# Order of work at three joints of a hybrid encoder kernel: scan entry, last routed tile, second expert block

## The chip, the core and the metric

The kernel runs on one core of a Trainium2 chip. A core has five engines with an instruction stream each: PE (TensorE, matrix products into PSUM), DVE (VectorE), ACT (ScalarE), POOL (GpSimd), and SP (SyncE), which here only issues DMA transfers. They meet through semaphores. All transfers are carried by the core's 16 DMA engines; SP's go through one queue (q1), POOL's indirect gathers and scatters through another (q0). The metric is device time in microseconds, the median of several executions, less is better.

## The reference

Two batches, of 1024 and 512 tokens with 1024 features in float32, pass one layer each with shared weights; the kernel treats them as 1536 tokens in 12 tiles of 128.

```python
def _forward(x, ...):
    h = _rms_norm(x, norm1_w)
    u = h @ w_in
    y_a = _rwkv7_mixer(shifted u, ...)        # 8 heads x 64, both directions
    y_b = _hgrn2_mixer(u, lb, gnorm_w)        # 4 heads x 128, both directions
    x = x + concat(y_a, y_b) @ w_out
    h2 = _rms_norm(x, norm2_w)
    x = x + _hier_moe(h2, ...)
    return _rms_norm(x, final_norm_w)

# hgrn2, per direction, chunks of 32 steps
    G = jnp.cumsum(g_c, axis=-2)
    o = A @ v_c + (q_c * jnp.exp(G)) @ S      # A: decayed scores inside a chunk
    S = jnp.exp(G_last)[..., None] * S + (k_c * jnp.exp(G_last - G)).T @ v_c

# hier_moe
    glog = h @ wg + bg ; grp = argmax(glog)
    elog = h @ we + be ; top_v, top_i = top_k(elog of that group, 2)
    # rows sorted by expert into blocks of 128, then for each block
    hid = silu(xb @ w_gate[e]) * (xb @ w_up[e]) ; yb = hid @ w_down[e]
    # gate-weighted sum of the two experts of each token
```

## The kernel before

It is one program in stages. First the input projection of the RWKV columns, with norm and token shift. Then `mix_rwkv_project_hgrn`: the RWKV recurrence over 48 chunks of 32 steps (iteration `c` of `steps()`), interleaved on PE with the projection of the HGRN2 columns. This stage is a block of its own: its five engine programs end together, and the next block's begin together. The next block is `mix_hgrn_project_out` with the routing and, without another such border, `experts_and_final_norm`.

**The scan entry.** At the end of the RWKV block SP loads the chunks' decays (`scan_decay`) and the first tile's keys and queries (`kq_first`) back from DRAM; DVE makes the products of decays of the HGRN2 scan (`upto`, `to2`, `to3`) and the first tile's scaled keys (L1540 to L1566). The scan itself goes over 12 tiles with index `c`, for two directions `d`. Its steps are `prep` (DVE scales keys), `scores` (PE), `turn_k` (PE turns the keys, ACT copies them), `grow` (PE multiplies keys by values, DVE adds this to the state) and `out` (PE, two products for each of four heads, into `o_ps_o`). Each engine runs its own version of the step. `schedule` fixes one order for all engines, and `gap(c, budget)` puts pieces of other work (`fillers`: norms, gates, output projection, routing) between them: r_ names belong to the RWKV half, n_ names to the norm of heads, `half` to the output projection, and `turn`, `routed`, `choose`, `rank`, `place` to the router.

**The last routed tile.** A finished tile n (order `FINISHED`) goes through: `half` x 4 (two column halves of `ps_out`, two parts of the sum), `x1_half` (DVE adds the residual), `x1` (ACT squares), `msq`, `m_root`, `h2n` (DVE scales the tile by the root and the norm weight into `work`), `turn` x 2 (PE turns it through `ps_x`, ACT copies to `h2T`), `routed` (PE, eight products with the router weights; DVE adds the bias). For each pair g of tiles `choose` picks the experts, `weigh` makes the exponentials, `rank` counts on PE and `place` gives each row its slot. POOL scatters the tokens to the `slots`. After the last pair a single product with the matches gives the first block's row indices (`first_idx`).

**The expert blocks.** Block b takes 128 rows x[b % 2]. PE does gate (L2858), down of block b-1 (L2867), up (L2858). Weights are double-buffered: wg, wu, wd with index b % 2. Those of expert 0 and the gate weights of expert 1 are loaded when the scan ends. SP loads up and down of expert 1 after the first rows have landed (`e_first_row`), then goes through a loop in which each load waits for PE's last use of its buffer. POOL gathers rows: it waits for the scattered slots, loads the tokens of the block, and issues four indirect gathers of a quarter row each; DVE turns the block (L2971).

## Time and profile before

| | us |
|---|---|
| median of 3 runs | 2351.63 (2350.96 to 2352.99) |
| the profiled execution | 2347.96 |
| its span in the trace | 2346.1 |
| PE busy in the span | 2228.4 (95%) |
| DVE, ACT, POOL busy | 1032.1, 713.7, 407.5 |
| mean granted clock of TensorE | 0.978 of full speed |

The span is cut by the stages: RWKV projection to 360, RWKV recurrence to 1230, scan with output projection and routing to 1622, experts to 2318, final norm to the end. "Granted clock" is the share of TensorE's full 2.4 GHz; 0.5 is 1.2 GHz. In timelines a row is a run of equal instructions on one engine: start, length, what it is, and in brackets how long the engine was idle before it and whose work ended that idle time. A matmul in float32 leaves two records, so x8 are four matmuls.

### The profile page before, as it was taken

How to read it: one execution, taken by the hardware profiler on the slowest of the kernel's cores; microseconds unless marked ns; L12 is line 12 of the kernel's file. 1: busy time of each engine (PE TensorE's matmuls, PEld its weight loads, DVE VectorE, ACT ScalarE, POOL GpSimd, SP SyncE). 2: the span in 40 equal slices, each digit the busy share in tenths (PEclk: the TensorE clock that was granted, in tenths of full speed). 3: DMA queues.
4: the chain of work that ended last, by engine and by line, in shares of the span. 5: the costliest groups of instructions: out<-in, count | busy, mean ns of one | idle time of the engine just before them, and what ended most of it. 6: DMA issues, size and time to landing. Idle time of an engine off the chain costs nothing. (4 is left out here: it accounts for less than half of the span.)

```text
span 2346.1 us, 64499 instructions
## 1 busy us (share of the span) xinstructions
PE 2228.4 (95%) x28004; PEld 1463.3 (62%) x28004; DVE 1032.1 (44%) x2219; ACT 713.7 (30%) x1441; POOL 407.5 (17%) x506
## 2 busy tenths in 40 slices
PE   7999999999999999999998989998799999999996
PEld 4444444445555555555557756656688888888884
DVE  3336776834644744644655766644111111111114
ACT  4124454623544544544542322221000000000003
POOL 1012222310000000000002210102533333333321
PEclk9999999999999999999997999997899999999998
DMA  4103344443343333333338843454799999999997
GB/s 142 36 23 126 135 157 139 171 106 92 92 111 83 99 97 93 93 96 91 88 108 243 260 147 117 158 180 146 252 362 353 331 355 334 361 352 334 362 330 290
DMA packets 359966, 436.66 MB, mean 186 GB/s; under 512 B 164994, under 2 KB 296198, under 8 KB 351536
## 3 DMA queue, kind: packets, MB, share of 16 engines
q1 hardware_dynamic: 343232, 397.94, 50.0%
q0 software_dynamic: 14384, 35.19, 6.1%
q8 instruction: 192, 3.15, 0.6%
q10 hardware_dynamic: 2112, 0.01, 0.1%
q14 instruction: 46, 0.38, 0.0%
HBM read 329.84 MB, written 104.50 MB: 185 GB/s over the span
## 5 line engine op out<-in xcount | busy, mean ns | idle before, releaser
L1198 PE MATMUL h_pp<-hT,r_wcol 128*128 128x512 f32 x832 | 413.0, 619 | 3.3 <-ACT h_iraw L1313 3.3
L2858 PE MATMUL e_ps_gu<-e_xT,e_wg 128*128 128x128 f32 x2048 | 236.4, 277 | 12.6 <-DVE e_xT L2971 12.6
L2858 PEld LDWEIGHTS e_ps_gu<-e_xT,e_wu 128*128 128x128 f32 x2048 | 233.6, 192 | 14.3 <-issue 14.3
L2858 PEld LDWEIGHTS e_ps_gu<-e_xT,e_wg 128*128 128x128 f32 x2048 | 233.5, 194 | 13.2 <-DVE e_xT L2971 12.8
L2858 PE MATMUL e_ps_gu<-e_xT,e_wu 128*128 128x128 f32 x2048 | 233.8, 275 | 0.0
L2867 PE MATMUL e_ps_y<-e_wd,e_hid 128*128 128x512 f32 x512 | 225.1, 592 | 0.7 <-DVE e_hid L3030 0.7
L1198 PEld LDWEIGHTS h_pp<-hT,r_wcol 128*128 128x128 f32 x832 | 141.5, 189 | 124.0 <-issue 108.8
L522 PE MATMUL h_pp<-hT,r_wcol 128*128 128x512 f32 x480 | 215.2, 607 | 1.3 <-DVE hT L794 1.3
L2983 DVE TENSOR_SCALAR e_y<-e_ps_y,e_row 128x512 f32<-128x512 f32 x31 | 23.3, 751 | 337.7 <-PE e_ps_y L2867 337.6
L522 PEld LDWEIGHTS h_pp<-hT,r_wcol 128*128 128x128 f32 x480 | 92.6, 195 | 113.7 <-issue 112.0
L2867 PEld LDWEIGHTS e_ps_y<-e_wd,e_hid 128*128 128x128 f32 x512 | 94.8, 190 | 108.7 <-issue 107.1
L2922 ACT ACTIVATE e_silu<-e_ps_gu 128x512 f32<-128x512 f32 x31 | 18.5, 597 | 424.2 <-PE e_ps_gu L2858 424.2
L2255 PE MATMUL o_ps_out<-o_wout,y 128*128 128x512 f32 x288 | 130.6, 600 | 4.0 <-DVE y L2469 4.0
L2651 POOL DMA_INDIRECT e_x<-h,e_idx x128 | 124.6, 973 | 55.6 <-issue 29.3
L2010 POOL MEMSET g_mask<- 128x256 f32 x1 | 0.3, 311 | 736.8 <-POOLq L1058 736.8
L1375 ACT ACTIVATE m_v<-m_ps_x 32x256 f32<-32x256 f32 x192 | 72.0, 375 | 148.9 <-PE m_ps_x L1258 147.2
L2990 DVE TENSOR_TENSOR e_hid<-e_ps_gu,e_silu 128x512 f32<-128x512 f32 x31 | 21.4, 690 | 196.9 <-PE e_ps_gu L2858 196.9
L776 POOL TENSOR_TENSOR r_spans<-r_spans 128x512 f32<-128x512 f32 x24 | 42.0, 1770 | 375.5 <-DVE r_spans L866 375.5
L522 PE MATMUL r_pp<-hT,r_wcol 128*128 128x512 f32 x240 | 105.4, 592 | 0.0
L2255 PEld LDWEIGHTS o_ps_out<-o_wout,y 128*128 128x128 f32 x288 | 53.0, 192 | 60.7 <-issue 60.7
L522 PEld LDWEIGHTS r_pp<-hT,r_wcol 128*128 128x128 f32 x240 | 45.4, 190 | 56.4 <-issue 56.4
L2918 ACT ACTIVATE e_y<-e_ps_y,e_row 128x512 f32<-128x512 f32 x31 | 21.3, 687 | 185.8 <-PE e_ps_y L2867 185.8
(419 smaller groups left out, 3406.7 us busy)
## 6 DMA issues: line engine op xcount, KB each, us to landing
e_wg<-in_moe_w_gate_dram SPq DMA_DIRECT2D x32, 2048.0 KB, 12.6
e_wu<-in_moe_w_up_dram SPq DMA_DIRECT2D x32, 2048.0 KB, 12.8
e_wd<-in_moe_w_down_dram SPq DMA_DIRECT2D x32, 2048.0 KB, 12.7
r_wcol<-in_w_in_dram SPq DMA_DIRECT2D x35, 512.0 KB, 5.5
ar<-r_ar SPq DMA_DIRECT2D x24, 512.0 KB, 2.7
kb<-r_kb SPq DMA_DIRECT2D x24, 512.0 KB, 2.8
m_ar<-ar SPq DMA_DIRECT2D x48, 256.0 KB, 4.7
m_kb<-kb SPq DMA_DIRECT2D x48, 256.0 KB, 3.5
```

The lines of the kernel that those rows point to most:

```text
L522: last = nc.tensor.matmul(pp[k % SPANS][:], wcol[q][:, c], self.hT[:, c, s * SPAN:(s + 1) * SPAN], start=c == 0, stop=c == KT - 1)
L776: nc.gpsimd.tensor_tensor(gx[d][:], gi[d][:], sg[d][:], ALU.subtract).then_inc(*pool_aux.inc(f"gx{d}"))
L1198: last = nc.tensor.matmul(pp[n % 2][:], wcol[(k + 2) % 3][:, c], self.hT[:, c, span(s)], start=c == 0, stop=c == KT - 1)
L1375: last = nc.scalar.activation(out, ps_ru[quad[q]], ACT.Copy)
L2255: last = nc.tensor.matmul(ps_out[:, h * SPAN:(h + 1) * SPAN], y[:, k, tile(FINISHED[n])], wout[:, k, h * SPAN:(h + 1) * SPAN], start=k == ...
L2651: self.nc.gpsimd.indirect_dma_start(self.e_x[u][:, g], None, self.h2.rearrange("t (q e) -> (t q) e", q=4), bass.IndirectOffsetOnAxis(ap=se ...
L2858: last = nc.tensor.matmul(ps[:, q * P:(q + 1) * P], w[u][:, c, q * P:(q + 1) * P], xT[u][:, c * P:(c + 1) * P], start=c == 0, stop=c == KT ...
L2867: last = nc.tensor.matmul(ps_y[:, n * 512:(n + 1) * 512], hid[u][:, q * P:(q + 1) * P], wd[u][:, q, n * 512:(n + 1) * 512], start=q == 0, ...
L2918: return nc.scalar.activation(y[u][:, 0:512], ps_y[:, 0:512], ACT.Copy, scale=gate[u])
L2922: made = nc.scalar.activation(silu[:], ps_g, ACT.Silu)
L2983: return nc.vector.tensor_scalar(y[u][:, 512:], ps_y[:, 512:], gate[u], None, ALU.mult)
L2990: made = nc.vector.tensor_tensor(hid[u][:], ps_u, silu[:], ALU.mult)
```

## The change

Four edits.

1. The scan entry moves forward. SP's loads stand in `load_entry`, called right behind the last stores of keys and decays, ahead of later stores. DVE's instructions stand in `enter_scan`, called in the last chunk's iteration ahead of the last addition to the state.
2. At the scan's start, `prep(1)` stands ahead of the second `turn_k`, and the first tile's two `out` steps stand in front of the second `scores`. PE waits for the clearing of `ps_s` before its first scores, no longer at the block's top.
3. The order of the fillers for tile index 11 is written out in `endings()`. The last tile is not scaled by its root before it is turned: DVE multiplies each half by the norm weight as soon as it is added, and the root scales the logits in the instruction that adds the bias; ACT squares the halves apart (DVE adds the two sums) and scales `work` for the store of h2. After the scan the second half of each `turn` goes through `ps_k`, and `routed` begins when the first half is copied.
4. SP waits for the second block's rows as well before it loads up and down of expert 1.

```diff
+                    def load_entry():
+                        for u in range(2):
+                            sp.wait_ge(kq_stored[u], 16 * 3 * PAIRS)
+                            sp.wait_ge(dc_stored[u], 16 * PAIRS)
+                        sp.dma_start(scan_decay[:], self.hdecay.rearrange("d j p c -> p (d j) c")).then_inc(scan_decay_loaded, 16)
+                        for i in range(2):
+                            sp.dma_start(kq_first[:, i], self.kq.rearrange("d j two p t -> p two (d j) t")[:, i, :, 0:P]
+                                         ).then_inc(self.kq_loaded[0], 16)
...
                             if it == whole(m) + 5:
                                 store_kq(m, 2)
                                 store_dc(m)
+                                if m == 2 * PAIRS - 1:
+                                    load_entry()
...
+                    def enter_scan():
...
+                        nc.vector.memset(to3[:], 1.0).then_inc(spread, 1)
+                        eng.wait_ge(scan_decay_loaded, 16)
...
+                        if c == CHUNKS - 1:
+                            enter_scan()
                         if has_c:
                             self.waits(eng, pe_c.at("MO", c))
...
-                for n in range(-2, TILES + 3):
+                for n in range(-2, TILES - 1):
...
+                return out + endings()
+
+            def endings():
+
+                e, g = TILES - 1, LAST_PAIR - 1
+                return [(name, args, cost, e) for name, args, cost in (
+                    ("turn", (e - 2, 0), 1.1), ("rank", (g - 1,), 0.4), ("half", (e, 0, 0), 3.5), ("place", (g - 1,), 0),
+                    ("msq", (e - 1,), 0), ("m_root", (e - 1,), 0), ("turn", (e - 2, 1), 1.1), ("routed", (e - 2,), 1.7),
+                    ("h2n", (e - 1,), 0), ("half", (e, 1, 0), 3.5), ("choose", (g, 0), 0), ("turn", (e - 1, 0), 1.1),
+                    ("choose", (g, 1), 0), ("turn", (e - 1, 1), 1.1), ("half", (e, 0, 1), 3.5), ("routed", (e - 1,), 1.7),
+                    ("x1_half", (e, 0), 0), ("choose", (g, 2), 0), ("weigh", (g,), 0), ("half", (e, 1, 1), 3.5),
+                    ("x1_half", (e, 1), 0), ("x1", (e,), 0), ("msq", (e,), 0), ("rank", (g,), 0.4), ("turn", (e, 0), 1.1),
+                    ("turn", (e, 1), 1.1), ("m_root", (e,), 0), ("place", (g,), 0), ("h2n", (e,), 0), ("routed", (e,), 1.7))]
...
+                run("prep", 1)
                 run("turn_k", 0, 1)
+                run("out", 0, 0)
                 run("grow", 0, 1)
-                run("prep", 1)
                 gap(-1, 1.0)
+                run("out", 0, 1)
...
+            turn_bank = lambda n, h: bank_k if ("turn", n, h) in bank_k.use else bank_x
...
-                self.waits(eng, bank_x.done(("turn", n, 1)), bank_y.free(("logits", n)), (params, 16 * 5))
+                self.waits(eng, bank_y.free(("logits", n)), (params, 16 * 5))
                     for c in range(KT):
+                        if c % PAIRS == 0:
+                            self.waits(eng, turn_bank(n, c // PAIRS).done(("turn", n, c // PAIRS)))
...
+                def routed(n):
+                    if n == LAST:
+                        self.waits(eng, dve_t.at("inv", n))
+                        nc.scalar.activation(work[n % RING_X][:], work[n % RING_X][:], ACT.Copy, scale=rq[:, n:n + 1]
+                                             ).then_inc(*act_last.inc("h2"))
...
+                    if n == LAST:
+                        half = slice(h * SPAN, (h + 1) * SPAN)
+                        self.waits(eng, dve_x.at("x1" if h else "low", n))
+                        nc.vector.tensor_tensor(by_k(work[u][:, half]), hgrn(t) if h else rwkv(n), by_k(n2w[:, half]), ALU.mult
+                                                ).then_inc(*dve_last.inc("high" if h else "low"))
...
+                    if n == LAST:
+                        self.waits(eng, dve_t.at("inv", n))
+                        nc.vector.scalar_tensor_tensor(self.logits[:, FINISHED[n]], ps_y[:, 0:NG + NE], rq[:, n:n + 1], rbias[:],
+                                                       ALU.mult, ALU.add).then_inc(bank_y.read, 1)
+                        return
...
-                self.waits(sp, (self.e_first_row, 16))
+                self.waits(sp, (self.e_first_row, 16), (x_loaded[1], 64))
                 self.load_up(sp, 1, 1)
                 self.load_down(sp, 1, 1)
```

How this moves instructions on the engines, at three places. On DVE at the end of the RWKV block (`m_grown` and `m_state` are the addition to the last chunk's state; `g_to`, `g_upto`, `h_first` the scan entry), before:

```order
L1517 TENSOR_TENSOR m_xt<-m_px,m_ps_b 128x128
L1497 TENSOR_TENSOR m_grown<-m_ps_x,m_state 128x2x4x64
L1500 TENSOR_TENSOR m_state<-m_grown,m_decay 128x512
L1540 MEMSET g_to 128x384
L1542 MEMSET g_decay 128x8
L1544 COPY g_upto<-g_decay 128x96
```

And the end of the same stretch in the changed kernel:

```order
L1509 TENSOR_TENSOR h_first<-h_first,g_to 128x1024
L1512 TENSOR_TENSOR g_upto<-g_upto,g_decay 128x96
L1514 TENSOR_TENSOR g_upto<-g_upto,g_decay 128x96
L1516 TENSOR_TENSOR g_upto<-g_upto,g_decay 128x96
L1536 TENSOR_TENSOR m_grown<-m_ps_x,m_state 128x2x4x64
L1539 TENSOR_TENSOR m_state<-m_grown,m_decay 128x512
L1058 UNCONDITIONAL_BRANCH
```

The addition to the state is now the last work of the block, and the 14 instructions of the entry stand in front of it. On PE at the start of the scan (`e_wu`, `e_wg`, `e_wd` are the expert buffers, which hold values, state and keys during the scan; numbers are buffers), before, from the last first-tile scores on:

```order
L2200 MATMUL o_ps_s<-h_first 128x32 x8
L2214 MATMUL o_ps_k<-e_wu0,e_wg1 128x128 x4
L2207 MATMUL o_ps_k<-ident,h_first 128x128 x4
L2214 MATMUL o_ps_k<-e_wu0,e_wg1 128x128 x4
L2192 MATMUL o_ps_s<-e_wg0 32x32 x3
```

And after:

```order
L2231 MATMUL o_ps_s<-h_first 128x32 x8
L2245 MATMUL o_ps_k<-e_wu0,e_wg1 128x128 x4
L2238 MATMUL o_ps_k<-ident,h_first 128x128 x4
L2255 MATMUL o_ps_o<-e_wu0,e_wd0 128x128
L2257 MATMUL o_ps_o<-e_wg1,e_wu0 128x128
L2255 MATMUL o_ps_o<-e_wu0,e_wd0 128x128
L2257 MATMUL o_ps_o<-e_wg1,e_wu0 128x128
L2255 MATMUL o_ps_o<-e_wu0,e_wd0 128x128
L2257 MATMUL o_ps_o<-e_wg1,e_wu0 128x128
L2255 MATMUL o_ps_o<-e_wu0,e_wd0 128x128
L2257 MATMUL o_ps_o<-e_wg1,e_wu0 128x128
L2245 MATMUL o_ps_k<-e_wu0,e_wg1 128x128 x4
```

The first output (eight matmuls) stands between the second turn of the keys and the second growth; eight more for the other direction follow this growth, ahead of the second scores. On PE at the end of the routing (`o_ps_out` the output projection, `o_ps_y` logits and ranks, `o_ps_x` and `o_ps_k` turned halves), before:

```order
L2255 MATMUL o_ps_out<-o_wout,y 128x512 x8
L2264 MATMUL o_ps_x<-ident,o_x 128x128 x4
L2255 MATMUL o_ps_out<-o_wout,y 128x512 x8
L2271 MATMUL o_ps_y<-o_wr,o_top 128x36 x8
L2264 MATMUL o_ps_x<-ident,o_x 128x128 x8
L2271 MATMUL o_ps_y<-o_wr,o_top 128x36 x8
L2264 MATMUL o_ps_x<-ident,o_x 128x128 x4
L1680 MATMUL o_ps_y<-q_picked,q_strict 128x64
L1681 MATMUL o_ps_y<-q_before,allsum 128x64
L2264 MATMUL o_ps_x<-ident,o_x 128x128 x4
L2271 MATMUL o_ps_y<-o_wr,o_top 128x36 x8
```

And after:

```order
L2286 MATMUL o_ps_out<-o_wout,y 128x512 x4
L2296 MATMUL o_ps_k<-ident,o_x 128x128 x4
L2305 MATMUL o_ps_y<-o_wr,o_top 128x36 x8
L2286 MATMUL o_ps_out<-o_wout,y 128x512 x4
L2296 MATMUL o_ps_x<-ident,o_x 128x128 x4
L2296 MATMUL o_ps_k<-ident,o_x 128x128 x4
L2286 MATMUL o_ps_out<-o_wout,y 128x512 x4
L2305 MATMUL o_ps_y<-o_wr,o_top 128x36 x8
L2286 MATMUL o_ps_out<-o_wout,y 128x512 x4
L1688 MATMUL o_ps_y<-q_picked,q_strict 128x64
L1689 MATMUL o_ps_y<-q_before,allsum 128x64
L2296 MATMUL o_ps_x<-ident,o_x 128x128 x4
```

The router products and turns of the two tiles before stand between the projection's halves instead of behind them; only a turn of `o_ps_k` and the last router product follow these rows.

## Rows read from the trace of the kernel before

**Rows 1.** By stretch: us, busy of each engine (instructions), PE clock, DMA share, GB/s.

```profile
1300.00:1596.00 296.00, 281.03 (x1874) 187.83 (x1868) 176.78 (x464) 80.68 (x172) 37.77 (x34) 0.99 0.52 165
1600.30:1622.10 21.80, 17.83 (x84) 16.48 (x83) 14.28 (x78) 5.02 (x12) 4.65 (x12) 0.57 0.21 74
1657.35:2318.00 660.65, 660.06 (x4470) 540.14 (x4470) 115.04 (x113) 53.22 (x90) 233.71 (x304) 1.00 0.93 338
```

**Rows 2.** Timeline of DVE at the scan entry: start, length, work [idle before <-releaser].

```profile
1222.69 0.69 DVE L1497 TENSOR_TENSOR m_grown<-m_ps_x,m_state 128x512 f32<-128x512 f32 x1 [6.51 <-PE m_ps_x L1271]
...
1224.14 0.38 DVE L1540 MEMSET g_to<- 128x384 f32 x1
...
1228.81 0.33 DVE L1566 TENSOR_TENSOR g_upto<-g_upto,g_decay 128x96 f32<-128x96 f32 x1
```

**Rows 3.** Timeline of SP at the scan entry.

```profile
1205.70 0.47 SPq L1136 DMA_DIRECT2D hdecay<-h_dc  x1
...
1216.60 0.37 SPq L1170 DMA_DIRECT2D g_decay<-hdecay  x1
...
1227.76 0.34 SPq L1125 DMA_DIRECT2D hgate<-h_gst  x1
```

**Rows 4.** Timeline of PE in the first tiles of the scan.

```profile
1237.43 1.44 PE L2214 MATMUL o_ps_k<-e_wu,e_wg 128*128 128x128 f32 x8 [0.39 <-DMA e_wu<-itok]
1240.08 1.11 PE L2207 MATMUL o_ps_k<-ident,h_first 128*128 128x128 f32 x4 [1.22 <-DVE e_wg L2419]
1241.88 2.07 PE L2214 MATMUL o_ps_k<-e_wu,e_wg 128*128 128x128 f32 x8 [0.69 <-ACT e_wg L2302]
1247.29 0.33 PE L2192 MATMUL o_ps_s<-e_wg 128*32 128x32 f32 x6 [3.33 <-issue]
...
1255.27 0.63 PE L2224 MATMUL o_ps_o<-e_wu,e_wd 128*128 128x128 f32 x2
...
1258.64 1.06 PE L2214 MATMUL o_ps_k<-e_wu,e_wg 128*128 128x128 f32 x8
```

**Rows 5.** Timeline of PE near the end of the routing.

```profile
1584.36 7.09 PE L2255 MATMUL o_ps_out<-o_wout,y 128*128 128x512 f32 x16
...
1598.59 1.87 PE L2271 MATMUL o_ps_y<-o_wr,o_top 128*128 128x36 f32 x16
```

**Rows 6.** Timeline of DVE at the end of the routing.

```profile
1598.86 0.69 DVE L2481 TENSOR_TENSOR y<-o_ps_out,o_x 128x512 f32<-128x512 f32 x1 [2.74 <-PE o_ps_out L2255]
...
1608.49 0.23 DVE L1696 TENSOR_TENSOR q_pos<-o_ps_y,q_region 128x64 f32<-128x64 f32 x1 [1.21 <-PE o_ps_y L1681]
...
1610.84 0.16 DVE L1724 TENSOR_TENSOR q_token<-q_token,q_e 128x2 f32<-128x2 f32 x1
...
1614.00 0.16 DVE L1619 TENSOR_REDUCE q_gmax<-logits 128x2 f32<-128x8 f32 x1
```

**Rows 7.** Timelines of DVE and PE at the second expert block.

```profile
1655.28 2.01 DVE L2971 STREAM_TRANSPOSE e_xT<-e_x 128x1024 f32<-128x1024 f32 x1 [24.56 <-DMA e_x<-h,e_idx]
...
1657.35 9.31 PE L2858 MATMUL e_ps_gu<-e_xT,e_wg 128*128 128x128 f32 x64 [12.60 <-DVE e_xT L2971]
...
1680.51 7.31 PE L2858 MATMUL e_ps_gu<-e_xT,e_wg 128*128 128x128 f32 x64
```

**Rows 8.** Timelines of POOL and SP ahead of it.

```profile
1634.84 2.08 POOL L2639 DMA_DIRECT2D e_tok<-slots  x3 [6.20 <-DMA slots<-q_token,dest]
1641.36 0.18 POOL L2644 COPY e_row<-e_tok 128x4 uint32<-128x4 uint32 x1 [4.44 <-DMA e_tok<-slots]
...
1626.88 0.33 SPq L2615 DMA_DIRECT2D e_wu<-in_moe_w_up_dram  x1
```

**Rows 9.** Landings: slots 1550:1620; rows 1640:1648; rows 1657.5:1664.

```profile
DMA to landing us min/median/max: 2.1/2.1/4.1
...
DMA to landing us min/median/max: 4.4/7.0/8.6
...
DMA to landing us min/median/max: 2.7/2.7/2.7
```

More of the change, by code:

```diff
@@ L1975, in schedule @@
                     gap(c - 1, budget)
-                    run("out", c, 0)
+                    if c:
+                        run("out", c, 0)
                     if more:
@@ L1981, in schedule @@
                         run("turn_k", c + 1, 1)
[L1982 removed]
+                    if c:
+                        run("out", c, 1)
                     if c + 2 < TILES:
@@ L2099, in load_x @@
                         if n >= EARLY:
-                            self.waits(sp, bank_x.full(("turn", n - RING_X, 1)), (h2_stored[u], n // RING_X * 16))
+                            self.waits(sp, turn_bank(n - RING_X, 1).full(("turn", n - RING_X, 1)), (h2_stored[u], n // RING_X * 16))
                         elif n >= RING_X:
@@ L2352, in turn @@
                 def turn(n, h):
-                    self.waits(eng, bank_x.full(("turn", n, h)), bank_y.full(("logits", n - 1)))
-                    nc.scalar.activation(h2T[:, h * SPAN:(h + 1) * SPAN], ps_x[:], ACT.Copy).then_inc(bank_x.read, 1)
-                schedule(turn_k=turn_k, out=out, n_sq=n_sq, n_root=n_root, n_wide=n_wide, r_evict=r_evict, x1=x1, m_root=m_root, turn=turn,
+                    self.waits(eng, turn_bank(n, h).full(("turn", n, h)), bank_y.full(("logits", n - 1)))
+                    nc.scalar.activation(h2T[:, h * SPAN:(h + 1) * SPAN], turn_ps(n, h), ACT.Copy
+                                         ).then_inc(turn_bank(n, h).read, 1)
+                def routed(n):
[3 more added lines that the diff above has]
+                                             ).then_inc(*act_last.inc("h2"))
+                schedule(turn_k=turn_k, out=out, n_sq=n_sq, n_root=n_root, n_wide=n_wide, r_evict=r_evict, x1_half=x1_half, x1=x1, m_root=m_root, turn=turn, routed=routed,
                          weigh=lambda g: self.weigh(eng, g))
```

113 lines of the change are left out of this document (62 added, 51 removed).

## The prediction

> **What bounds the kernel now.** I read the page first: PE is busy 95% of the span, so a change can only give time where PE waits, or where it runs at half of its clock. Then I read PE's timeline and the waits of three places, and for each place the engine that ends the wait. After 1657.35 the expert loop runs without a hole: 660.06 of 660.65 us busy at a granted clock of 1.00, that is 2.4 GHz, with the DMA engines at a share of 0.93 [rows 1]. The change touches three joints ahead of this loop.
>
> *Scan entry, 1227 to 1260.* DVE prepares the scan from 1224.14 to 1229.14 [rows 2]; SP's last issue of the old block ends at 1228.10 [rows 3]. The new block starts after that. PE then sits idle 1.22, 0.69 and 3.33 us between 1238.87 and 1247.29, 5.24 in all, and the same eight matmuls of L2214 take 2.07 us at 1241.88 and 1.06 at 1258.64: the first at 1.2 GHz, the second at 2.4 [rows 4].
>
> *End of the routing, 1599 to 1622.* PE is busy up to 1600, then at a mean clock of 0.57 [rows 1]. The last half of x1 is added at 1598.86, and DVE begins to choose the last pair's experts at 1614.00 [rows 6]: 14.45 us after that addition's end at 1599.55.
>
> *Second block's rows, 1644 to 1657.* PE ends the first up projection at 1644.75 and stands 12.60 us until the second block's rows are turned; the gate projection then takes 9.31 us where one in the loop takes 7.31 [rows 7]. The rows are late because each link of POOL's chain lands slowly: 6.20 us of waiting for the scattered slots, 4.44 for the tokens [rows 8], up to 8.6 for the gather [rows 9]. SP has the weights of expert 1, two transfers of 2.1 MB, in flight since 1626.88 [rows 8].
>
> **The sum, part by part.**
>
> *Entry: 4.5 us.* The same instructions stand on DVE, ahead of the last addition of the state. DVE was free there: it waited 6.51 us until 1222.69 [rows 2], so from 1216.18. The entry is 5.00 us long and would end at 1221.2, 1.5 us before it hurts. Its three loads move on SP's queue from behind the gate store (1216.60) to behind the last store of the decays (issued by 1206.17) [rows 3]; the next issue on that queue came 10 us later, so they land before DVE comes to them and hold nothing up. What ends last now is SP at 1228.10, so the block turns over 1.04 us sooner. PE no longer waits for the clearing before its first turn; that is worth nothing, since growing the state waits for the value rows, which land with 0.39 us of idle as the end of the chain [rows 4]. Then the order: the first outputs, eight pairs of matmuls, go into the holes. One such output took 3.37 us at half clock (1255.27 to 1258.64), the other half as long again at full clock, 1.8: 5.2 us leave the stretch behind the second scores. In front, with the 1.04 us taken off: growth ends at 1237.8, turn 1.22 later until 1240.1, output to 1243.5, growth 2.07 to 1245.6, second output 3.4 more to 1249.0; the scores begin 1.7 us later than at 1247.29. Net 3.5 at half clock throughout. Moving the scaling of the second keys ahead of the second growth is what permits it: DVE does it while PE outputs. If the dense outputs raise the clock early, as 128-wide matmuls did from 1255.27 on, the second output takes 1.8 and the gain is 5.1; the scores and the turn before 1255.27 fill 8 us at half clock, and if most of that halves too, 8.6. Against this stands the DMA, which fills that stretch. I take 4.5, near the lower case; ends 1.0 (the turnover alone) and 8.6.
>
> *End: 6.1 us.* PE's work before the last half of x1 is the same four halves of the projection (16 records in 7.09 us, two halves; 6.87 without the overlap at the end, so 3.44 each) and one turn of 0.45. Two router products of 1.7 (1.87 less the same overlap) [rows 5] and two more turns, which stood behind them, now stand between them. So the last projection ends at 1584.36 + 4 x 3.44 + 3 x 0.45 + 2 x 1.7 = 1602.9 instead of 1598.8. DVE adds (0.69) and multiplies by the norm weight (0.69): 1604.3. PE turns both halves at once, into two banks, unscaled. ACT squares the last half (by my estimate 0.6 with the sum behind it), then copies the two turns, loads its table and takes the root; DVE meanwhile places the older pair, 2.5 us (1608.49 to 1611.00 before) [rows 6], from 1604.9 to 1607.4, and I take the root to be there by then. One reciprocal and the scaled logits follow, 0.4: choosing begins at 1607.9 instead of 1614.00. The 2 x 0.69 on DVE and the whole-tile scaling on ACT are new; the latter feeds only the store of h2, which the first gather reads when choosing and ranking are over, as now. Ends: 4.0, if the root comes 2 us behind the placement; 7.5, if PE's clock, 0.57 in the mean there [rows 1], also stays up through the small products behind.
>
> *Rows before weights: 14.6 us.* SP now waits for the second rows before it issues expert 1's up and down weights. POOL's chain then meets idle DMA engines. I use the quiet landings, 2.1 us for slots and 2.7 for rows [rows 9]: POOL is free at 1628.64 (1634.84 - 6.20), slots there at 1630.7, tokens at 1633.5 (with 2.7 again), and the 13.92 us from 1641.36 to 1655.28 shrink by 8.6 - 2.7 to 8.0: rows there at 1641.5, turned 2.0 later at 1643.5 [rows 7, 8]. PE's up projection ends at 1644.75. So the wait goes whole, 12.60, and with it the cold start, 9.31 - 7.31 = 2.0. What is late next? SP's weights, issued at 1641.5 instead of 1626.9. The up weights are wanted after gate and down, 1644.75 + 7.15 + 6.87 = 1658.8; 2.1 MB at the loop's 338 GB/s [rows 1] take 6.2 us. The next gate weights stand behind 6.8 MB in all: 20.1 us, 1661.6, wanted at 1665.9. Later ones have more time. Queued behind SP's new wait are those loads only. Ends: 8.7, if the gather still lands in 8.6; 14.6, since no more hole is left.
>
> This case's landings speak to a rule. A gather took 4.4 to 8.6 us beside the weights and 2.7 alone [rows 9]. The Trainium skill, DMA: Bandwidth & Descriptors, section Queues, rings and completion order, says each DMA engine goes round-robin between queue rows at packet granularity; read strictly, a small transfer then never stands behind the whole 4 MB, and holding the weights back gives the rows little. By the rule the third term is near 0; by the rows it is 14.6. The trace bears the interleaving out in so far as the gather did land long before the weights' 4 MB were through, yet three times later than alone.
>
> All three move in a line (the second joint starts later work only by its own sum), and the entry's gain passes 1300 to 1596, where PE is busy all but 15 us of 296 [rows 1]. 4.5 + 6.1 + 14.6 = 25.2. The profiled execution took 2347.96 (span 2346.1), so 2322.8. It stood 3.67 below the median of the three runs, 2351.63; against that median I predict 2326.4.
>
> **Rivals.**
> *Entry absorbed:* the stretch is held by transfers (the value rows are the releaser at 1237.43), and the reordered outputs only move idle time. Entry 1.0, total 21.7: 2329.9.
> *Rows still late:* POOL's chain is slow for its own reasons, or packets interleave anyway. For it: POOL's own issues and three round trips are in it. Against: the quiet landings. Third term 0, total 10.6: 2341.0.
> *Weights late, slower:* the loop is transfer-bound at a share of 0.93, and the time in which no weights are issued never comes back. Place: the up weights of the second block and all behind them. If the rows came as late as 1655.28, issue slips by 28.4 us; less 10.6 that gives +17.8: 2369.4. It decides once the weights' lateness eats more than 10.6 us. Against it: PE lost 0.6 us in 660 at that share [rows 1].
> *Change not effective:* the entry's loads land late, DVE holds up the last state and the block; that costs what it exceeds 1.5 us by, at most about 3: 2326.4 + 7.5 = 2333.9.
>
> **Chances.** Forecast 0.66, entry absorbed 0.20, rows late 0.08, entry held up 0.03, weights late 0.03. The likeliest case alone ranges from 2321 to 2333. The range with eight in ten, 2320 to 2336, takes in the absorbed entry and a gather that lands half as slowly; it leaves out the late rows and late weights. 0.2% is 4.7 us, about what a measurement of this kernel can tell from no change. All cases but one are faster by more: faster 0.96, same 0.02, slower 0.02.
>
> **What would show it.** Entry: DVE's scan preparation ends near 1221, PE's holes of 1.22 and 3.33 are one of 1.2, and the second scores start between 1247 and 1249. End: from the last addition of x1 to the choosing, 4.3 us instead of 14.45. Rows: no PE idle before the second gate projection, that projection at 7.31, slots and tokens landing in 2 to 3 us. It is wrong if PE shows a wait on expert weights in the loop, if the gather still lands in over 6 us, or if PE's holes reappear between 1260 and 1300.

## The result and the profile after

| | before | changed |
|---|---|---|
| median of 4 runs, us | 2351.30 (2346.73 to 2352.99) | 2319.53 (2315.62 to 2324.88) |
| profiled execution, us | 2347.96 | 2317.24 |
| its span, us | 2346.1 | 2315.7 |
| mean granted clock of TensorE | 0.978 | 0.984 |

The ratio of the medians is 0.9869, with a 95% interval of 0.9843 to 0.9896: 24.5 to 36.9 us faster. The forecast was 2326.4 us, with a range of 2320 to 2336; the median lies 0.5 us under the low end. Two things have to be told apart: what the edits moved, and why the total is larger than that.

**Three joints.** I cut both traces at the same instructions. The scan stretch runs from the end of the last projection of the block before to the first half projection of the last tile; the end stretch from there to the choosing of the last pair's experts; the rows stretch from there to the first down projection of the experts.

| stretch, us | before | changed | gained | forecast |
|---|---|---|---|---|
| ahead of the scan | 1227.10 | 1221.72 | 5.38 | 0 |
| scan | 357.26 | 351.58 | 5.68 | 4.5 |
| end | 29.64 | 23.90 | 5.74 | 6.1 |
| rows | 52.49 | 38.61 | 13.88 | 14.6 |
| from there to the end | 679.62 | 679.84 | -0.22 | 0 |

The edits' stretches give 25.3 us where the forecast had 25.2. Most of the surplus is the first row. Here are the windows of both kernels up to the last projection (columns: stretch, its length, PE busy with its instructions, PE clock, DMA share, GB/s). First before:

```profile
0.00:1227.10 1227.10, 1182.44 (x20736) 0.99 0.37 104
```

then the changed kernel:

```profile
0.00:1221.70 1221.70, 1179.96 (x20736) 0.99 0.37 104
```

The same 20736 instructions, 2.5 us less of busy time and 2.9 us less of idle time. The first moved instruction in this stretch is SP's load of the decays, at 1203.01 in the changed kernel. Here is one group of 32 of PE's records well ahead of it, before and then changed:

```profile
1193.31 1.10 PE L1217 MATMUL m_ps_s<-m_ar,m_kb 64*64 64x128 f32 x32
```

```profile
1187.78 1.10 PE L1221 MATMUL m_ps_s<-m_ar,m_kb 64*64 64x128 f32 x32
```

The changed kernel is 5.53 us ahead there, and 5.38 at the end of the stretch. So the lead was there before any edited instruction ran, and the moved ones added nothing to it.

**Scan entry** [rows 2 to 4]. DVE's timeline in the changed kernel (start, length, work, [idle before <-releaser]):

```profile
1210.83 0.38 DVE L1490 MEMSET g_to<- 128x384 f32 x1
...
1215.52 0.33 DVE L1516 TENSOR_TENSOR g_upto<-g_upto,g_decay 128x96 f32<-128x96 f32 x1
1217.38 0.69 DVE L1536 TENSOR_TENSOR m_grown<-m_ps_x,m_state 128x512 f32<-128x512 f32 x1 [1.53 <-PE m_ps_x L1275]
```

The preparation takes 5.0 us and leaves 1.53 us before the state's last addition; 1.5 was forecast. SP's last old issue and its first new one:

```profile
1222.38 0.34 SPq L1125 DMA_DIRECT2D hgate<-h_gst  x1
1223.25 0.59 SPq L2106 DMA_DIRECT2D y<-ytok  x1
```

That store still ends last, as forecast. PE in the first tiles:

```profile
1223.28 0.63 PE L2238 MATMUL o_ps_k<-ident,h_first 128*128 128x128 f32 x4 [1.56 <-PEq L1058]
...
1230.74 2.05 PE L2245 MATMUL o_ps_k<-e_wu,e_wg 128*128 128x128 f32 x8 [2.02 <-DMA e_wu<-itok]
1234.00 1.12 PE L2238 MATMUL o_ps_k<-ident,h_first 128*128 128x128 f32 x4 [1.22 <-DVE e_wg L2470]
...
1236.62 0.45 PE L2255 MATMUL o_ps_o<-e_wu,e_wd 128*128 128x128 f32 x2
...
1237.58 1.06 PE L2245 MATMUL o_ps_k<-e_wu,e_wg 128*128 128x128 f32 x8
...
1241.60 1.12 PE L2228 MATMUL o_ps_s<-e_wg 128*64 128x32 f32 x16
...
1250.69 1.11 PE L2264 MATMUL o_ps_x<-ident,o_wide 128*128 128x128 f32 x4 [1.88 <-DVE o_wide L2503]
```

The holes of 0.69 and 3.33 us of [rows 4] are filled. The clock rises inside the first output (0.45 instead of 0.63 us for a matmul), so the second growth takes 1.06 and the second scores start at 1240.5: 18.75 us after the last projection's end, where the kernel before took 20.19 and I had forecast 20 to 22. The value rows are now waited for, 2.02 us, and a new hole of 1.88 stands at 1250.69.

**End of the routing** [rows 5, 6]. DVE, and then PE's last half projection:

```profile
1592.31 0.69 DVE L2532 TENSOR_TENSOR y<-o_ps_out,o_x 128x512 f32<-128x512 f32 x1 [0.95 <-PE o_ps_out L2286]
1593.04 0.69 DVE L2537 TENSOR_TENSOR o_x<-y,o_top 128x512 f32<-128x512 f32 x1
...
1596.39 0.16 DVE L1732 TENSOR_TENSOR q_token<-q_token,q_e 128x2 f32<-128x2 f32 x1
1596.62 0.16 DVE L2551 RECIPROCAL o_rq<-o_rq 128x1 f32<-128x1 f32 x1
1596.92 0.26 DVE L2562 SCALAR_TENSOR_TENSOR logits<-o_ps_y,o_rq,o_rbias 128x36 f32<-128x36 f32 x1
1597.21 0.16 DVE L1627 TENSOR_REDUCE q_gmax<-logits 128x2 f32<-128x8 f32 x1
```

```profile
1588.53 3.68 PE L2286 MATMUL o_ps_out<-o_wout,y 128*128 128x512 f32 x8
```

From the addition's end to the choosing 4.2 us; 4.3 was forecast, 14.45 stood there before. The reciprocal follows the placing of the older pair without a wait: the root had been ready.

**Second block's rows** [rows 7 to 9]. POOL, SP, DVE and PE in the changed kernel:

```profile
1613.29 2.08 POOL L2706 DMA_DIRECT2D e_tok<-slots  x3 [1.43 <-DMA slots<-q_token,dest]
1615.47 0.18 POOL L2711 COPY e_row<-e_tok 128x4 uint32<-128x4 uint32 x1
```

```profile
1623.60 0.33 SPq L2682 DMA_DIRECT2D e_wu<-in_moe_w_up_dram  x1
```

```profile
1623.53 2.04 DVE L3038 STREAM_TRANSPOSE e_xT<-e_x 128x1024 f32<-128x1024 f32 x1 [9.54 <-DMA e_x<-h,e_idx]
```

```profile
1628.67 7.31 PE L2925 MATMUL e_ps_gu<-e_xT,e_wg 128*128 128x128 f32 x64
1635.82 7.03 PE L2934 MATMUL e_ps_y<-e_wd,e_hid 128*128 128x512 f32 x16
1642.69 7.31 PE L2925 MATMUL e_ps_gu<-e_xT,e_wu 128*128 128x128 f32 x64
```

The wait for the slots fell from 6.20 to 1.43, that for the tokens from 4.44 to nothing; the slots' landing, from one tile's view of 1605 to 1616:

```profile
DMA to landing us min/median/max: 2.1/2.1/2.1
```

The rows are turned at 1625.6, 3.1 us before PE wants them. The windows of the changed kernel for the end of the routing and for the loop (busy of PE, weight load, DVE, ACT and POOL with their instructions, then clock, DMA share, GB/s) show the same pace of the loop as in [rows 1], at a slightly higher share of DMA:

```profile
1583.60:1605.40 21.80, 16.66 (x90) 12.19 (x88) 13.43 (x68) 9.07 (x17) 4.64 (x12) 0.84 0.16 50
...
1628.67:2287.60 658.93, 658.15 (x4473) 538.22 (x4471) 115.24 (x115) 53.44 (x90) 235.55 (x307) 1.00 0.96 352
```

### The profile page after: what moved, and what is told of

Same layout as the page of the kernel before. It is cut to its first block and busy times, and to the rows that moved or that the text cites. A ratio compares the mean times of both kernels' runs of the same rounds, so it can differ in the third digit from the quotient of the medians.

```text
span 2315.7 us, 64509 instructions
## 1 busy us (share of the span) xinstructions
PE 2215.1 (96%) x28004; PEld 1453.8 (63%) x28004; DVE 1032.3 (45%) x2221; ACT 717.5 (31%) x1446; POOL 407.9 (18%) x506
## 5 line engine op out<-in xcount | busy, mean ns | idle before, releaser
L2989 ACT ACTIVATE e_silu<-e_ps_gu 128x512 f32<-128x512 f32 x31 | 18.5, 597 | 410.3 <-PE e_ps_gu L2925 396.6
```

## The experiments

All were timed beside the kernel before, in four sessions (1 to 4, 5 to 8, 9 to 11, and 12; the kernel before had medians of 2350.24, 2347.85, 2346.57 and 2350.60 there); each ratio is to the kernel before of its session. A profile is one execution; in experiments 3, 4 and 8 it was the slowest of its kernel. "Scan", "end" and "rows" are the stretches above in the profiled execution, and "lead" is the end of the last projection ahead of them.

| run | median, us | ratio (95%) | lead | scan | end | rows |
|---|---|---|---|---|---|---|
| before, first profile | 2351.30 | 1 | 1227.10 | 357.26 | 29.64 | 52.49 |
| changed, first profile | 2319.53 | 0.9869 (0.9843 to 0.9896) | 1221.72 | 351.58 | 23.90 | 38.61 |
| 1 changed again | 2319.99 | 0.9881 (0.9861 to 0.9900) | 1222.45 | 352.54 | 23.90 | 38.88 |
| 2 weights first | 2336.24 | 0.9948 (0.9929 to 0.9966) | 1228.77 | 353.22 | 23.90 | 51.05 |
| 3 outputs back | 2326.68 | 0.9901 (0.9883 to 0.9919) | 1227.92 | 363.21 | 23.90 | 38.35 |
| 4 preparation back | 2322.04 | 0.9883 (0.9865 to 0.9900) | 1228.67 | 355.39 | 23.90 | 37.88 |
| 5 endings back | 2326.57 | 0.9909 (0.9884 to 0.9934) | 1224.32 | 356.43 | 28.46 | 37.43 |
| 6 before, rows first | 2334.45 | 0.9949 (0.9932 to 0.9967) | 1221.11 | 361.62 | 29.61 | 37.76 |
| 7 up weights first | 2325.39 | 0.9904 (0.9879 to 0.9930) | 1223.33 | 353.90 | 23.90 | 42.30 |
| 8 values first | 2323.08 | 0.9894 (0.9867 to 0.9920) | 1230.24 | 356.96 | 23.90 | 37.53 |
| 9 fill rows | 2321.10 | 0.9888 (0.9863 to 0.9914) | 1223.72 | 353.04 | 23.90 | 38.64 |
| 10 fill both | 2323.85 | 0.9894 (0.9865 to 0.9924) | 1225.99 | 352.39 | 23.90 | 38.69 |
| 11 fill scan | 2322.43 | 0.9899 (0.9872 to 0.9925) | 1221.49 | 354.64 | 23.90 | 37.97 |
| 12 whole entry back | 2330.62 | 0.9913 (0.9883 to 0.9944) | 1228.19 | 356.81 | 23.90 | 38.54 |

**1, the changed kernel again** (no edit).

> The changed kernel once more, unedited. In its first profile the three joints gave 5.7 (scan entry), 5.7 (end of routing) and 13.9 us (second block's rows), 25.3 in all, and 5.4 us more stood ahead of the first edited instruction: the last projection of the block before the scan ended 5.38 us earlier on the span's clock. Theory A (those 5.4 us are scatter of a single execution): in this profile the three joints give 5 to 6, 5 to 6 and 13 to 15 again, the 5.4 comes out as any number between -4 and +6, and the median stands 24 to 28 us below the kernel before. Theory B (the edits speed the program up from its start, by where its code or its tiles lie): the last projection is again 5 us early, and the median stands 30 to 32 us below.

The joints came out as 4.7 (357.26 - 352.54), 5.7 and 13.6 us. The lead was again early, 1222.45, and the median 30.3 us under the kernel before, which by itself spoke for theory B. The later runs overturned it. Experiments 2 and 3 have the same instructions up there and led at 1228.77 and 1227.92; experiment 6, which is the kernel before up to its expert block, led at 1221.11. The four leads without the moved preparation have a mean of 1226.3, the ten with it 1225.0, each scattering over 7 us or more. Whole executions of one kernel differ as much: 2344.23 to 2354.41 us for the kernel before where it was timed beside experiments 1 to 4. Theory A; a part of 1.3 us, the difference of the means, can't be told from nothing.

**2, weights first.**

```
-                self.waits(sp, (self.e_first_row, 16), (x_loaded[1], 64))
+                self.waits(sp, (self.e_first_row, 16))
```

> The changed kernel with one wait taken back: SP issues expert 1's up and down weights after the first row again. Forecast's theory (bytes in flight slow the small transfers): slots, tokens and gather land in some 6, 4.4 and 4.4 to 8.6 us again, PE stands 12 us before the second gate projection and runs it in 9.3 us: 13.9 us slower than the changed kernel. Rival (packets interleave between queue rows, the small ones never stand behind 4 MB, and the gain came from elsewhere): within 2 us of the changed kernel.

POOL and PE in its trace:

```profile
1626.92 2.08 POOL L2706 DMA_DIRECT2D e_tok<-slots  x3 [6.37 <-DMA slots<-q_token,dest]
1632.66 0.18 POOL L2711 COPY e_row<-e_tok 128x4 uint32<-128x4 uint32 x1 [3.66 <-DMA e_tok<-slots]
```

```profile
1647.91 9.20 PE L2925 MATMUL e_ps_gu<-e_xT,e_wg 128*128 128x128 f32 x64 [10.41 <-DVE e_xT L3038]
```

The rows stretch is 12.4 us longer than in the changed kernel (13.9 was expected), the median 16.3 above experiment 1 of the same session. The forecast's theory holds, the rival falls.

**3, outputs back.** The changed kernel's first-tile order undone:

```
                 run("grow", 0, 0)
-                run("prep", 1)
                 run("turn_k", 0, 1)
-                run("out", 0, 0)
                 run("grow", 0, 1)
+                run("prep", 1)
                 gap(-1, 1.0)
-                run("out", 0, 1)
...
-                    if c:
-                        run("out", c, 0)
+                    run("out", c, 0)
...
```

> The changed kernel with the first tile's two outputs and the scaling of the second keys back in their old places; the moved scan entry stays. The scan entry's joint gave 5.7 us in the first profile. Theory A (holes and clock: the outputs fill PE's 1.2 and 3.3 us of waiting and raise the clock early): 4.7 us slower than the changed kernel, with holes of 1.2 and 3.3 us and the second scores at half clock in the trace. Theory B (transfers hold the stretch until 1280, the outputs only move idle time): under 1.5 us slower.

The median is 6.7 us above experiment 1. The waits of PE in the 80 us behind the last projection (engine, line, <- waited for: us in total, times, longest) begin with the hole that the outputs had filled:

```profile
PE o_ps_s L2219 <- issue: 4.5, 2, 3.3
...
PE o_ps_k L2241 <- DMA e_wu<-itok: 1.7, 1, 1.7
```

In the changed kernel there is no wait before the scores but 0.7 us at the block's start.

Theory A in kind, with the second scores at half clock as it says. The scan stretch of this execution, 363.21, overstates it: the profiled execution was the slowest of its runs (2334.81 us), and experiment 12 shows the same order at 356.81.

**4, preparation back.** The three loads and DVE's preparation stand again behind the loop; the outputs stay moved:

```
-                        if c == CHUNKS - 1:
-                            enter_scan()
...
-                                if m == 2 * PAIRS - 1:
-                                    load_entry()
```

> The changed kernel with the scan entry (DVE's preparation and its three loads) back behind the loop of the block before; the outputs stay moved. Theory A (the entry is worth the turnover alone): 1.0 us slower than the changed kernel, 7.1 us instead of 6.1 from the start of the last projection matmul to the scan's first load on SP. Theory B (the later turnover is absorbed by the value rows, which PE waits for): 0 to 0.3 us, since these rows are issued by the block's own first instructions that is unlikely. Theory C (the order of loads around the gate store also mattered): over 2 us.

From the end of the last projection to PE's first turn it took 2.59 us instead of 1.56, which is the 1.0 of theory A. The median is 2.1 us above experiment 1, with intervals that overlap almost whole; by the medians 1.0 cannot be told from 0 or 2. Theory C, over 2 us, is not excluded by them either; a steadier point in the stretch is read below experiment 12.

**5, endings back.** The last tile as every other:

```
-                return out + endings()
+                return out
...
-            LAST = TILES - 1
+            LAST = None
...
-            turn_bank = lambda n, h: bank_k if ("turn", n, h) in bank_k.use else bank_x
+            turn_bank = lambda n, h: bank_x
...
```

> The changed kernel with the last tile treated as every other again (old end order, one bank for the two turns, norm ahead of the turns). Forecast's theory: from the end of the last addition of x1 to the choosing of the last pair 14.4 us instead of 4.2, while the last projection ends some 4 us earlier; net 5.7 us slower than the changed kernel. Rival (the wait moves: without the new order the ranking and the slots hide part of it): under 3 us slower.

The end stretch is 4.6 us longer (28.46 against 23.90), the median 6.6 above experiment 1's 2319.99 of the other session. From addition to choosing 13.3 us, not 14.4: the mean clock over that time was 0.71 there, 0.63 in the kernel before. The rows stretch is 1.2 shorter than in the changed kernel, since the first gate projection ran less of its time at half clock (7.56 us against 8.62); by both stretches together it is 3.4. So the forecast's theory holds in kind, and the rival, under 3 us, misses by little: up to the choosing the edit is worth 4.6 against this run and 5.7 against the kernel before and experiment 6, and a part of that goes again in the first gate projection.

**6, the kernel before with rows first.** The reverse of experiment 2, on the kernel before.

> The kernel before with one wait added: SP issues expert 1's up and down weights only when the second block's rows have landed. Forecast's theory: this part alone is worth what it was worth with the others, 12 to 14.5 us faster than the kernel before, no idle time of PE before the second gate projection, that projection at 7.3 us. Rival (it pays only after the other two edits, since they moved the rows): under 8 us faster.

```profile
1642.96 7.31 PE L2858 MATMUL e_ps_gu<-e_xT,e_wg 128*128 128x128 f32 x64
```

No idle time ahead of it. The rows stretch shrank by 14.7 us (52.49 to 37.76) and the median by 13.4 (2347.85 to 2334.45). The part is worth as much alone as beside the others, within what the runs can tell, and the rival, under 8 us, falls.

**7, up weights first.**

```
-                self.waits(sp, (self.e_first_row, 16), (x_loaded[1], 64))
+                self.waits(sp, (self.e_first_row, 16))
                 self.load_up(sp, 1, 1)
+                self.waits(sp, (x_loaded[1], 64))
                 self.load_down(sp, 1, 1)
```

> The changed kernel with half of the held weights let go: expert 1's up weights (2.1 MB) are issued after the first row, the down weights still wait for the second rows. Theory A (what delays the small transfers is the bytes queued at that moment, about 6 us of transfer for 2.1 MB): the slots land late (wait of 4 to 6 us instead of 1.4), tokens and gather land as in the changed kernel, the rows are turned 3 to 4 us later, which the up projection just covers: 0 to 1.5 us slower than the changed kernel. Theory B (any weight transfer in flight slows every link, whatever its size): rows 8 us late or more, over 5 us slower. Theory C (packets interleave, nothing is delayed): no link changes.

```profile
1622.07 2.08 POOL L2706 DMA_DIRECT2D e_tok<-slots  x3 [6.30 <-DMA slots<-q_token,dest]
1624.38 0.18 POOL L2711 COPY e_row<-e_tok 128x4 uint32<-128x4 uint32 x1 [0.23 <-DMA e_tok<-slots]
```

```profile
1634.55 5.69 PE L2926 MATMUL e_ps_gu<-e_xT,e_wg 128*128 128x128 f32 x34 [2.46 <-DVE e_xT L3039]
```

PE and the DMA engines in slices of 2.5 us (slice, length, PE busy with its instructions, PE clock, DMA share, GB/s):

```profile
1617.00:1619.50 2.50, 2.50 (x17) 0.75 0.97 407
1619.50:1622.00 2.50, 2.50 (x25) 1.00 0.77 322
1622.00:1624.50 2.50, 2.50 (x25) 1.00 0.18 6
```

Issued at 1614.00, the 2.1 MB are through at about 1622, and the slots, issued by 1615.8, land with them; tokens and gather then land as in the changed kernel. That is theory A's mechanism. Its price was too low: the rows came 5 us later, not 3 to 4, so PE stood 2.46 us and ran a part of the projection at half clock (9.04 us for the whole of it, where the changed kernel takes 7.31); the rows stretch grew by 3.7 us. Theory C falls. Theory B falls by the links, of which only one was slowed, and by the rows, 5 us late and not 8; by the median alone, 5.4 us above experiment 1's of another session, it could not be told from A.

**8, values first.**

```
-                load_y(0)
                 load_v(0)
+                load_y(0)
```

> The changed kernel with two loads at the start of the scan block swapped: the value rows, for which PE waited 0.4 us before and 2.0 us after the change, are issued ahead of the first tile's y and bonus rows. Theory A (PE's wait at the first growth is the order of these loads): the value rows are issued 1.3 us sooner, the 2.0 us wait shrinks to 0.7 or less, 1.3 to 2.0 us faster than the changed kernel. Theory B (the y rows, now later, hold the normalising that PE waits for around 1250): the time comes back as a longer wait there, within 0.5 us of the changed kernel.

```profile
1237.07 1.14 PE L2245 MATMUL o_ps_k<-e_wu,e_wg 128*128 128x128 f32 x8
...
1251.27 1.65 PE L2245 MATMUL o_ps_k<-e_wu,e_wg 128*128 128x128 f32 x8 [1.83 <-DMA e_wu<-itok]
...
1259.19 1.22 PE L2245 MATMUL o_ps_k<-e_wu,e_wg 128*128 128x128 f32 x4 [2.24 <-ACT e_wg L2336]
```

The first wait is gone and the first growth starts 6.83 us after the last projection instead of 9.01. Then 1.83 us are waited for the second tile's values and 2.24 for a copy of ACT. In this execution the time came back, though at other waits than theory B named: the fourth tile's scores started 54.0 us behind the last projection, 52.3 in the changed kernel. The median, 2323.08, is no gain, so theory A falls.

**9 and 10, idle matmuls against the half clock.** In 9 they stand ahead of the wait for the first expert's rows; 10 has 16 more (into another bank) ahead of the last ranking:

```
+                for i in range(20):
+                    nc.tensor.matmul(ps_g[:, i % 4 * P:(i % 4 + 1) * P], self.ident[:], self.ident[:], start=True, stop=True)
                 self.waits(eng, (self.e_first_row, 16))
```

> The changed kernel with 20 idle matmuls (identity by identity, 128x128, into a bank that the first gate projection overwrites later) at the start of the expert block, where PE waits 4.9 us for the first expert's rows with its clock at 1.2 GHz. They change no output. Theory A (the half clock of the first gate projection, 8.6 us where one at 2.4 GHz takes 7.15, comes from PE's idle time before it): the clock is up when the rows land, their turning takes 1.0 instead of 2.0, the table 0.5 instead of 1.1, the first gate projection 7.15: up to 3 us faster than the changed kernel, and no more, since the second rows are turned 3.0 us before the first up projection ends. Theory B (the dummies outlast the wait, at half clock 20 of them take 5 us): same or up to 1 us slower.

> As the kernel with 20 idle matmuls ahead of the first expert's rows, and 16 more in the 3.7 us in which PE waits for the last choosing, ahead of the ranking. Theory A: the clock does not fall at the end of the routing, ranking, counting and the last sum of the row numbers (0.66 + 0.63 + 0.58 + 1.01 us at half clock) take half as long; 1.4 us more than the other, some 4 us in all faster than the changed kernel; but the second rows come 1.4 us sooner as well, so nothing is newly late. Theory B (these small matmuls are bound by their latency, not by the clock): no more than the other kernel.

PE in experiment 9:

```profile
1608.59 7.36 PE L2942 MATMUL e_ps_gu<-ident 128*128 128x128 f32 x40
1615.78 1.05 PE L2945 MATMUL e_ps_y<-ident,e_x 128*128 128x128 f32 x8
...
1617.76 7.41 PE L2925 MATMUL e_ps_gu<-e_xT,e_wg 128*128 128x128 f32 x64 [0.38 <-DVE e_xT L3045]
```

and in experiment 10:

```profile
1604.81 5.74 PE L2325 MATMUL o_ps_x<-ident 128*128 128x128 f32 x32
1610.39 0.33 PE L1688 MATMUL o_ps_y<-q_picked,q_strict 128*128 128x64 f32 x2
```

In 9 the clock was up for the turning (1.05 us, 1.97 in the changed kernel) and the first gate projection (7.41 instead of 8.62), but the 20 dummies, 40 records, ran 7.36 us, 2.5 longer than the wait they filled. The rows stretch stayed at 38.64. In 10 ranking took 0.33 instead of 0.66, so theory B there (latency, not clock) falls; but the clock had fallen before the dummies began (0.50 from 1602.0 to 1604.8), stayed down for 4 us of them, and their 5.74 us again outlasted the 3.70 us wait. In 9, theory A is right on the clock and theory B on the outcome; fewer dummies were not tried.

**11, fill scan.** Twelve such matmuls behind the first scores.

> The changed kernel with 12 idle matmuls (identity by identity) behind the first scores, where PE waits 2.0 us for the value rows ahead of the first growth, which then runs at half clock (2.05 instead of 1.06 us), as do the turn (1.1 instead of 0.65) and four of the eight output pairs (0.43 instead of 0.22 each). Theory A (clock): these 2.4 us go, less what the dummies outlast the wait: 0 to 2.4 us faster. Theory B (the stretch until 1300 is held by transfers, as the swap of the loads showed, where 2.0 us saved at the first growth came back at the second tile's values): within 0.5 us of the changed kernel at 1305.

```profile
1225.93 1.92 PE L2228 MATMUL o_ps_s<-h_first 128*64 128x32 f32 x16
1227.78 3.62 PE L2231 MATMUL o_ps_s<-h_first 128*128 128x32 f32 x16
1231.22 4.71 PE L2236 MATMUL o_ps_x<-ident 128*128 128x128 f32 x24
1235.76 1.06 PE L2249 MATMUL o_ps_k<-e_wu,e_wg 128*128 128x128 f32 x8
```

Here the clock fell ahead of the scores already (1.92 and 3.62 us, where they took 1.12 and 1.97), so the dummies were slow too and growth began 5.3 us later than in the changed kernel. Yet at the seventh tile's scores only 1.2 us of lateness were left, counted from the last projection (102.4 against 101.1 us). That is neither theory's number: the delay of 5.3 us at the front was mostly swallowed, as the 2.2 us gain of experiment 8 was. What happens before 1250 goes on down this stretch only in part.

**12, whole entry back.** The edits of 3 and 4 together, with the clearing waited for at the block's start again.

> The changed kernel with both edits of the scan entry undone (preparation and its loads behind the block before, first tile's outputs and the scaling of the second keys in their old places); the end of the routing and the held weights stay. From the end of the last projection ahead of the scan to the first of the last tile's four half projections the profiles show 357.3 and 361.6 us without the entry's edits, and 351.6, 352.5, 353.2, 353.9 and 356.4 with them, apart from kernels that alter this stretch. Theory A (the entry is worth what these means say): 359.4 against 353.5, so about 6 us slower than the changed kernel. Theory B (the forecast's rival, the entry is absorbed by transfers and the first profiles were lucky): under 2 us slower, and that stretch at 354 us or less. Theory C (the two edits overlap, since the outputs back alone cost 6.7 us by the medians and the moved preparation 2.1): more than 8 us.

The scan stretch is 356.81, with the old waits: 3.8 us for the preparation, 4.5 us of issue. With the kernel before and experiment 6 that makes 357.26, 361.62 and 356.81, mean 358.6, without the entry's edits; with them and otherwise unaltered in this stretch 351.58, 352.54, 353.22, 356.43, 353.90, 353.04 and 352.39, mean 353.3. The two groups do not overlap, by 0.4 us. The entry is worth 5.3 us by the means. Theory B falls.

The start of the fourth tile's scores, counted from the end of the last projection, says where. It comes after 57.6, 58.8 and 56.3 us in the three kernels without the entry's edits and after 51.1 to 53.8 in the seven with them: 5.5 us sooner by the means. With the outputs back alone (experiment 3) it comes after 56.0, outside the seven; with the preparation back alone (experiment 4) after 52.9, inside them. So the outputs carry most of the gain, and it is there by the fourth tile. Experiment 3's stretch is 6.4 us longer than experiment 12's, and all of it comes behind this point, where the two kernels do the same. Nothing here shows theory C: with both edits back the point comes 0.3 us later than with the outputs back alone. The medians leave it open: 10.6 us above experiment 1's, in another session, and by the two ratios, 0.9913 and 0.9881, 7.5.

## Why the prediction was right, and where it was not

- *Entry, 4.5 forecast, 5.7 in the pair of profiles, 5.3 by the means.* The turnover was right to 0.02 (1.04 forecast, 7.11 to 6.09 from the start of the last projection's matmuls to SP's first load; experiment 4 takes it back). The order of the outputs was right in kind and under-sized: the sum of 3.5 counted half clock throughout, and the clock rose in the first output, the case that I had named beside it (5.1). It does not in every execution: in experiment 9 it rose only in the second growth, 1.85 us long. At the third tile's scores the changed kernel is 7.0 us ahead of the kernel before, counted from the last projection (31.7 against 38.7), at the fourth's 5.3: from the one to the other it took 20.5 us at a mean clock of 0.91, the kernel before 18.9 at 1.00. So a part of what the clock gave in front goes again there. Of the 5.68 us, 2.7 are shorter busy time (327.13 to 324.44) and 3.0 shorter idle time; I had counted mostly idle time. My line that not waiting for the clearing is worth nothing, since growing waits for the values, held nearly: PE's first turn starts 1.56 us behind the last projection instead of 3.80, and the wait for the values, 2.02 instead of 0.39, takes most of this back, so growth starts 1.3 us sooner where 1.04 was forecast. What I had at nothing was that growth now runs at half clock: 2.05 us instead of 1.44. The windows of PE over the scan stretch, before:

```profile
1227.10:1584.36 357.26, 327.13 (x2509) 0.96 0.59 183
```

and changed:

```profile
1221.72:1573.30 351.58, 324.44 (x2509) 0.97 0.60 186
```

- *Entry absorbed, given 0.20.* It fell as a whole, but its mechanism is there in part: experiments 8 and 11 moved the front by -2.2 and +5.3 us, and by the fourth tile's scores the one was 1.7 later and the other 0.4 earlier than the changed kernel. Their whole stretches, 5.4 and 3.1 us longer, say less, being single executions in a scatter of 5. That transfers do the absorbing is shown only in part: of the two waits read in experiment 8, 1.83 us were for a load and 2.24 for ACT. The signs named as proof of error partly came: new waits of 1.88 and 1.63 us stand at 1250 to 1260 in the changed kernel, none over 1.22 from 1260 to 1300.
- *End, 6.1 forecast, 5.74 at the choosing.* The last projection ended 18.9 us after the first half projection started; 18.5 was forecast. The chain behind was right to 0.1 us. I had not foreseen what came behind it: PE is now idle 3.7 us ahead of the last ranking (1.1 before), and ahead of the first rows 4.9 as before (4.8), and the first gate projection ran at a mean clock of 0.56 in its first 3 us: 8.62 us where it took 7.80. The size is that of one pair of executions. This projection took 7.47 to 8.97 us in the nine executions with the new end and no dummies ahead of it, 8.3 in the mean, and 7.56 to 7.82 in the three with the old one, 7.7 in the mean. That the longer idle time is the reason is likely and not shown.
- *Rows, 14.6 forecast, 13.9 measured.* Wait and cold start went whole, 12.60 and 2.0, and the slower first gate projection took 0.8 back. Experiments 2 and 6 give 12.4 and 14.7 for the same edit, taken back alone and made alone. Of the landings that I borrowed, 2.1 us was right for the slots, and the tokens landed in 2.1 too, where I had taken 2.7. The gather was there at 1623.5, 1.8 us after its last issue ended, and the rows were turned 3.1 us ahead of need, forecast 1.3. No PE wait on expert weights appeared: the up weights issued at 1623.60 were used at 1642.69 without a wait.
- *The rule on queues* (Trainium skill, DMA: Bandwidth & Descriptors, Queues, rings and completion order) would have put this term near 0. Experiments 2 and 7 decide against its strict reading for this case: with 2.1 MB in flight the slots' wait was 6.30 us, with 4.2 MB 6.37, with none 1.43. The size in flight did not lengthen that single wait; it decided how many of the following links were hit: with 2.1 MB the tokens were waited for 0.23 us, with 4.2 MB 3.66.
- *The total.* 25.2 forecast, 25.3 by the stretches, 31.8 by the medians. That the sum of the three comes out to 0.1 is in part luck: they miss by +1.2, -0.4 and -0.7. The step that failed is the one from the profiled execution to the median: I took before's place, 3.67 under its median, for both kernels, while the changed kernel's profiled execution lay 2.3 under its own, and its lead was 5.4 us shorter. In the pair of profiles the 5.4 us stand ahead of every edit. By the runs, the lead alone scatters from 1221.1 to 1230.2 for the same projection, and the scan by 5 us more. Whether the 5 to 6 us of the medians beyond the stretches are such scatter is open. For it: 25.3 lies inside both intervals (24.5 to 36.9, and 23.5 to 32.7 in experiment 1), and experiments 9 to 11, each of whose stretches equals the changed kernel's within 3.1 us, had medians only 22.7 to 25.5 us under the kernel before of their session. Against it: two sessions agree on 30 to 32.

## What to carry over

Before large prefetches are issued, look for a chain of small dependent transfers that starts at the same moment: hold the large ones until the chain has landed, if the engines they feed have work meanwhile, and check that work's length against their transfer time. Here the whole of it was worth 12 to 15 us, and one early transfer of 2.1 MB gave back 3.7 of that. And when a sum of local terms is compared with a median, compare the stretches ahead of the first edit too: here they differed by 5.4 us, as much as either of the two smaller terms.

## What was not expected

- TensorE's half clock comes in single stretches inside the scan, at places that change from execution to execution. Some follow a wait: in the kernel before the mean was 0.53 from 1365 to 1368, behind 3.92 us of idle time, and 0.50 from 1403 to 1405, behind 3.32. Others do not: in experiment 5 it was 0.56 from 1452 to 1455 with PE busy throughout, and PE had not been idle since a wait of 0.78 us that ended at 1441.05. In the changed kernel the mean from 1350 to 1360 was 0.52, with PE busy 6.66 of the 10 us; the turns at 1349.36 and 1350.22 were slow already (1.07 and 1.06 us, where one at 2.4 GHz took 0.63), ahead of the 3.35 us wait inside that stretch.
- PE multiplied identities without a break and the clock stayed at 1.2 GHz for the first 5.5 us of them in experiment 9 and for the first 4 in experiment 10. Filling a wait of 3.7 or 4.9 us at half clock therefore brought the clock up only when the wait was over.
- A version that beats the changed kernel was not found: none of experiments 7 to 11 has a lower median.
